# Moving the scan's states, the values' transposes and a modulation panel within the first block of a two-block kernel

## The chip, the cores and the metric

The kernel runs on one core of a Trainium2 chip. The metric is the device time of one execution in microseconds (us). Times below come from one profiled execution or from the timed runs, and the text says which. TensorE is called PE, its weight loads PEld, VectorE DVE, ScalarE ACT, GpSimd POOL; SP is the engine that issues the DMAs of the weights.

## What is computed

The program chains two blocks. The change is in the first, a hybrid layer over 512 tokens of width 1024 with a context of 256 tokens: a modulated norm, one projection, neighbourhood attention and a bidirectional state-space scan side by side, an output projection and a gated feed-forward part. Cut to what the change touches:

```python
mod = silu(c) @ ada_w + ada_b                  # six vectors of 1024: shifts, scales, gates
p = h @ w_in                                   # columns q, k, v | z | xbc | dt
attn = neighbourhood_attention(q, k, v, kc, vc, rpb, rows)   # softmax over a window and the context
dt = softplus(dt_raw + dt_bias);  a = -exp(a_log)            # step sizes, rates
xbc = silu(depthwise_conv(xbc));  xs, bm, cm = split(xbc)
# the scan, in chunks of 128, forward and backward:
cum = cumsum(dt * a);  w_end = exp(cum[-1] - cum) * dt
states = einsum("jgn,jge,jgep->gepn", bm, w_end, xs)         # one per chunk and direction
h = exp(cum[-1]) * h + states                                # carried from chunk to chunk
y = (cb * decay * dt) @ xs + (cm * exp(cum)) @ h_in;  y = rms_norm((y + d * xs) * silu(z))
x = x + g1 * (concat(attn, y) @ w_out);  x = x + g2 * conv_glu(modulate(rms_norm(x)))
```

## The kernel before

**Panels.** Every weight matrix is cut into panels of 128 columns. A panel is loaded by DMA into one of three raw buffers, ACT writes its high part (`wh`, L653), DVE or POOL the rest (`wl`, L663), and PE forms three products for each of 8 slices of the contraction (high x high, high weights x low input, low weights x high input; L685), so 24 products a panel. Panels alternate between two weight slots and two pairs of accumulator banks; ACT or DVE takes the sum out of PSUM. The low part is first needed by the third product. In the first block come 4 panels q, 4 k, 4 v, 1 dt, 8 xbc, 4 z (the gate), then 8 wo (the output projection).

**Modulation.** The 32 panels of the modulation weights that aren't needed at the start travel in the same stream of raw buffers, one behind each projection panel (`panels_of`, two behind dt). POOL multiplies and adds one (four instructions, L972 to L981), or DVE from number 24 on (eight instructions, L958 and L961, `mod_by`); its column sum (`modset`, L865) is done by PE two panels later. A raw buffer is loaded again when its reader is done, and SP issues the loads in the order of the stream.

**One plan, five streams.** `put` appends steps to one list, `plan`; afterwards each engine runs over that list and emits its own part of every step, with waits on semaphores. So the order within an engine is the order of `put`, and an instruction that waits holds all behind it on its engine. Small results use a ring of four banks (4 to 7) or of eight.

**Work beside the panels.** `gemm(..., every=5)` calls `tick` at products 1, 6, 11, 16 and 21 of a panel. `tick` advances the generator `na_order`, which puts one step and yields. If it yields `ALONE`, the slot is full; otherwise `tick` is called once more. The 12 panels xbc and z hold 60 slots. `drain` runs what is left. `na_order` holds 16 units of attention (scores, turn of the probabilities, values), then the rates of the scan (`rates1`) and the silu of xbc (`silu_x`, two halves of 128 x 3076).

**Around it.** Behind dt PE turns the step sizes (`dt_turn`), softplus goes back and forth between DVE and ACT, and nine tiles of values are turned by PE (`turn_v`, L1123) and copied by ACT (L1264) into `V`. `V` lies where the step sizes' scratch `wdt` and `sp_t` lay, so its copies, and the DMA of the mask, wait for `sp_done`. `zero_pads` clears DVE's convolution buffers. Behind each xbc panel DVE runs a convolution (L1333 to L1338).

**The scan.** After z: `turn_s` turns a chunk's x and B (PE L1571, L1575; ACT copies them), `state` (PE L1589) multiplies B with x times the end weights (DVE L1738 forward, POOL L1910 backward), `run` (DVE L1746 to L1756) carries the state on into `Hst`. Ten states, six chunks (4 and 5 are the context). Then `prep` (PE L1599, L1606), `masked` and `yout` work off eight pairs of chunk and group; this stage is called the next stage below. `Hst` shares memory with the projection's inputs `hh` and `hl`, which z still reads.

Of the kernel before, what the change touches and what calls it, by code (L numbers as in the profile page):

```python
# [120 lines left out]
def program(nc, io):  # L121
    ctx = ExitStack()
    with ctx:
# [177 lines left out]
        def mod_by(n):  # L301
            return "mod_dve" if n >= 24 else "mod_part"
# [688 lines left out]
        wdt = sbt(sc, "wdt", [128, S + CT])  # L991
        sp_t = [sbt(sc, f"spt{i}", [128, 96]) for i in range(4)]
        sc.close()
        sc = ExitStack()
# [20 lines left out]
        def natural(src):  # L1015
# [4 lines left out]
            "softplus": "sp_in/0 sp_out/0 sp_in/1 sp_out/1 sp_done", "turn_v": "turned copied",  # L1020
            "na_scores": "biased scored maxed/0 maxed/1 exped/0 exped/1", "na_turn": "turned/0 turned/1 copied/0 copied/1 scaled",
            "na_values": "weighed copied scaled",
            "steps1": "act_fn scaled",
# [13 lines left out]
        def na_order():  # L1037
            for u in range(16 + 1):
# [14 lines left out]
            yield ALONE  # L1053
            yield ALONE
            put("silu_x", 1)
            yield ALONE

        gemm(("q",), then_first, feed=feed_first)
# [24 lines left out]
        def first_sync(sp, w):  # L1083
# [5 lines left out]
            def na_mask():  # L1089
                w.wait_ge(s.sp_done, at("sp_done", "softplus", 0))  # L1090
# [6 lines left out]
            return {"rope_tables": rope_tables, "na_mask": na_mask, "na_rel": na_rel}  # L1097

        def first_tensor(pe, w, held, free):
# [19 lines left out]
            def turn_v(i):  # L1119
                b, = bank("turn_v", i)  # L1120
                held(b)
                for m in range(4):
                    ins = pe.transpose(ps[b][:, 128 * m:128 * m + 128], vT[:, m, V_AT[i]:V_AT[i] + 128], C("ident"))  # L1123
                ins.then_inc(up("turned", "turn_v", i), 1)
                free[b] = [(s.copied, at("copied", "turn_v", i))]
# [26 lines left out]
            def na_values(u):  # L1152
# [8 lines left out]
                for k, v in enumerate((*VI[j], 7, 8)):  # L1161
                    for e in range(2):
# [5 lines left out]
            return {"rope": rope, "dt_turn": dt_turn, "turn_v": turn_v, "na_scores": na_scores, "na_turn": na_turn,  # L1168
# [37 lines left out]
        def first_scalar(ac, w):  # L1206
# [85 lines left out]
        def first_vector(dv, w, st):  # L1292
# [98 lines left out]
        Hst = sbt(sb_, "Hst", [128, 2, 4, 512])  # L1391
# [7 lines left out]
        CBm = [sbt(sb_, f"CBm{i}", [128, 2, 128]) for i in range(2)]  # L1399
        seg = [sbt(sb_, f"seg{i}", [128, 512]) for i in range(2)]  # L1400
        Ms = [sbt(sb_, f"Ms{i}", [128, 512]) for i in range(4)]
        Cs = [sbt(sb_, f"Cs{i}", [128, 512]) for i in range(4)]
        yt = sbt(sb_, "yt", [128, 2, 128])
# [5 lines left out]
        ORDERS = [[4, 5, 0, 1, 2, 3], [5, 4, 3, 2, 1, 0]]  # L1409
        TRI = ["upper", "lower"]  # L1410
        STATES = [(d, ORDERS[d][n], n == 0) for n in range(5) for d in range(2)]
# [2411 lines left out]
```

## Time and profile before

| | us |
|---|---|
| timed runs, median of 3 (lowest, highest) | 2633.28 (2632.15, 2634.3) |
| the profiled execution | 2630.9 |
| its span (first to last instruction) | 2628.9 |
| busy in the span: PE, PEld | 2488.0 (95%), 2203.1 (84%) |
| busy in the span: DVE, ACT, POOL | 1351.1 (51%), 973.6 (37%), 961.3 (37%) |

The profile page also draws the span in 40 slices of 65.7 us. Each digit is a busy share in tenths; PEclk is the clock granted to TensorE, in tenths of its upper level (2.4 GHz). The first block's projection, attention and scan lie in slices 2 to 7.

```profile
PE   7989988999999999999999999999998998999997
DVE  4646577644534544454364354466654534644453
PEclk9999999999999999999999999999999998999998
```

A busy share of 95% over the whole span says nothing of one stage. The timeline of an engine gives start, duration, instruction and, in brackets, the idle time before it and what ended that.

### The profile page before, as it was taken

The numbers are of one execution on the slowest core, as the hardware profiler recorded it, in microseconds if no ns is written. First come the engines' busy times: TensorE is split into PE (matmuls) and PEld (weight loads), VectorE is DVE, ScalarE is ACT, GpSimd is POOL, SyncE is SP. The second block draws the span as 40 slices with busy tenths as digits, with TensorE's granted clock in tenths as the row PEclk, the third lists the DMA queues.
The fourth block names the chain that finished last, engine by engine and source line by source line (L and its number), as shares of the span: only waits on it lengthen the run. The fifth ranks groups of instructions, "written<-read, shape, count | busy, mean of one in ns | idle before, by whom it ended". The sixth has DMA issues, their size and how long they took to land.

```text
span 2628.9 us, 44461 instructions
## 1 busy us (share of the span) xinstructions
PE 2488.0 (95%) x19232; PEld 2203.1 (84%) x19232; DVE 1351.1 (51%) x2057; ACT 973.6 (37%) x1558; POOL 961.3 (37%) x553
## 2 busy tenths in 40 slices
PE   7989988999999999999999999999998998999997
PEld 5877676788887878878999999988988987989896
DVE  4646577644534544454364354466654534644453
ACT  5244453322323443424433333354333234333332
POOL 1754443344445222212445454500002114454544
PEclk9999999999999999999999999999999998999998
DMA  8432212333333211111223332312111002232321
GB/s 247 135 103 77 71 41 81 96 90 95 96 92 93 57 41 49 41 44 39 81 73 106 87 97 79 95 49 65 35 40 33 22 24 71 81 106 87 104 76 62
DMA packets 379858, 201.26 MB, mean 77 GB/s; under 512 B 6400, under 2 KB 377088, under 8 KB 379664
## 3 DMA queue, kind: packets, MB, share of 16 engines
q1 hardware_dynamic: 379664, 198.42, 26.6%
q8 instruction: 152, 2.49, 0.4%
q14 instruction: 42, 0.34, 0.0%
HBM read 196.30 MB, written 2.10 MB: 75 GB/s over the span
## 4 chain that ended last, share of the span: by engine, by line
PE 61%; DVE 12%; ACT 5%; issue 2%; POOL 2%; POOLq 0%; ACTq 0%; DVEq 0%
PE ps L685 48%; DVE t_ffy L2953 3%; DVE t_atq L2747 2%; ACT t_wh L653 1%; PE ps L2555 1%; PE ps L3188 1%; PE ps L2528 1%; DVE t_ffy L2956 1%; PE ps L2494 1%; PE ps L3207 1%; ACT t_ffy L2856 1%; PE ps L3211 1%; POOL t_wl L663 1%; DVE t_ainv L2775 1%; DVE t_wl L663 1%
## 5 line engine op out<-in xcount | busy, mean ns | idle before, releaser
L663 POOL TENSOR_TENSOR t_wl<-t_raw,t_wh 128x1024 fp32r<-128x1024 f32 (+2 forms) x196 | 443.4, 2263 | 810.2 <-ACT t_wh L653 810.1
L685 PE MATMUL ps<-t_hh,t_wh 128*128 128x264 f32 (+2 forms) x1712 | 402.8, 314 | 12.1 <-DVE t_dcq L2681 3.6
L653 ACT ACTIVATE t_wh<-t_raw 128x1024 fp32r<-128x1024 f32 (+2 forms) x253 | 255.4, 1012 | 415.0 <-PE ps L685 368.3
L685 PE MATMUL ps<-t_hh,t_wl 128*128 128x264 f32 (+2 forms) x1712 | 379.6, 300 | 4.7 <-POOL t_wl L663 3.1
L685 PE MATMUL ps<-t_hl,t_wh 128*128 128x264 f32 (+2 forms) x1712 | 376.9, 301 | 0.0
L685 PEld LDWEIGHTS ps<-t_hh,t_wh 128*128 128x128 f32 x1712 | 269.9, 191 | 36.9 <-issue 19.8
L685 PEld LDWEIGHTS ps<-t_hh,t_wl 128*128 128x128 f32 x1712 | 269.9, 190 | 21.4 <-issue 6.5
L685 PEld LDWEIGHTS ps<-t_hl,t_wh 128*128 128x128 f32 x1712 | 269.3, 191 | 14.6 <-issue 7.1
L2953 DVE SCALAR_TENSOR_TENSOR t_ffy<-t_ffp,t_vec,t_ffy 128x528 f32<-128x528 f32 (+1 forms) x88 | 176.1, 2002 | 178.8 <-ACT t_ffy L2856 178.8
L663 POOL TENSOR_TENSOR t_fwl<-t_raw,t_fwh 128x1024 fp32r<-128x1024 f32 (+1 forms) x72 | 167.9, 2333 | 152.2 <-ACT t_fwh L653 152.2
L685 PE MATMUL ps<-t_fhh,t_wl 128*128 128x512 f32 (+1 forms) x704 | 210.9, 340 | 2.9 <-POOL t_wl L663 2.8
L685 PE MATMUL ps<-t_fhh,t_wh 128*128 128x512 f32 (+1 forms) x704 | 210.5, 340 | 1.9 <-DVE t_fhl L1850 1.9
L685 PE MATMUL ps<-t_fhl,t_wh 128*128 128x512 f32 (+1 forms) x704 | 208.1, 338 | 0.0
L685 PEld LDWEIGHTS ps<-t_fhh,t_wl 128*128 128x128 f32 x704 | 120.0, 188 | 20.6 <-POOL t_wl L663 4.8
L685 PEld LDWEIGHTS ps<-t_fhh,t_wh 128*128 128x128 f32 x704 | 120.1, 188 | 20.1 <-DVE t_fhl L1850 3.4
L685 PEld LDWEIGHTS ps<-t_fhl,t_wh 128*128 128x128 f32 x704 | 119.5, 188 | 16.7 <-issue 0.4
L2998 POOL TENSOR_TENSOR t_ffl<-t_ffy,t_ffh 128x528 fp32r<-128x528 f32 (+1 forms) x44 | 57.8, 1314 | 132.3 <-ACT t_ffh L2865 132.3
L2681 DVE TENSOR_TENSOR t_ffp<-ps,t_rstd 128x264 f32<-128x264 f32 (+2 forms) x176 | 67.1, 422 | 74.6 <-PE ps L685 74.2
L663 DVE TENSOR_TENSOR t_wl<-t_raw,t_wh 128x1024 fp32r<-128x1024 f32 x57 | 78.8, 1384 | 49.0 <-ACT t_wh L653 49.0
L2747 DVE RECIPROCAL t_atq<-t_atq 128x528 f32<-128x528 f32 x16 | 55.2, 3453 | 70.8 <-ACT t_atq L2615 70.8
L653 ACT ACTIVATE t_fwh<-t_raw 128x1024 fp32r<-128x1024 f32 (+1 forms) x72 | 73.7, 1024 | 41.6 <-PE ps L685 36.8
L3634 POOL TENSOR_TENSOR t_dq<-t_dq,t_dRr 128x512 f32<-128x512 f32 (+1 forms) x10 | 11.4, 1137 | 200.9 <-PE ps L3158 200.9
(571 smaller groups left out, 5426.3 us busy)
## 6 DMA issues: line engine op xcount, KB each, us to landing
t_raw<-in_up SPq DMA_DIRECT2D x44, 512.0 KB, 3.9
t_raw<-in_up2a SPq DMA_DIRECT2D x44, 512.0 KB, 3.9
t_raw<-in_up2b SPq DMA_DIRECT2D x44, 512.0 KB, 3.9
t_raw<-in_attn_in SPq DMA_DIRECT2D x33, 512.0 KB, 4.1
t_raw<-in_dn_in SPq DMA_DIRECT2D x33, 512.0 KB, 4.1
t_raw<-in_ada_w SPq DMA_DIRECT2D x32, 512.0 KB, 4.1
t_raw<-in_w_in SPq DMA_DIRECT2D x25, 512.0 KB, 4.3
t_raw<-in_down SPq DMA_DIRECT2D x16, 512.0 KB, 4.1
```

The lines of the kernel that those rows point to most:

```text
L653: ac.activation(wh[slot_of[j]][:, 0:kc, :], raw[r % NRAW][:, 0:kc, :], ACT.Copy).then_inc(up("wh_cut", "cut", j), 1)
L663: eng.tensor_tensor(wl[slot_of[j]][:, 0:kc, :], raw[r % NRAW][:, 0:kc, :], wh[slot_of[j]][:, 0:kc, :].bitcast(F), SUB).then_inc(up(name, " ...
L685: ins = pe.matmul(ps[bank_of(j, i)][:, 0:tn], wt[slot][:, k, :], a[:, k, t0:t0 + tn], start=first, stop=last)
L2494: pe.matmul(ps[b][0:tn, 0:wide], aq[p % 3][64 * e:64 * e + 64, t0:t0 + tn], ak[p % 3][64 * e:64 * e + 64, a:a + wide], start=True, stop=False)
L2528: pe.matmul(ps[b][0:tn, 0:wide], ak[p % 3][64 * e:64 * e + 64, t0:t0 + tn], aq[p % 3][64 * e:64 * e + 64, q0:q0 + wide], start=True, stop= ...
L2555: ins = pe.matmul(ps[b][64 * e:64 * e + 64, lo - q0:lo - q0 + n], lhs, pT[e][0:tn, P_AT[k] + lo - t0:P_AT[k] + lo - t0 + n], start=k == 0, ...
L2681: ins = dv.tensor_tensor(a[part_, t0:t0 + tn], ap[part_, :], rstd[part_, t0:t0 + tn], MUL)
L2747: dv.reciprocal(tq[m][:, :], tq[m][:, :]).then_inc(up("inverted", "pair_norm", p, m), 1)
L2775: dv.reciprocal(inv[:, :], ps[bs_][:, 0:wide]).then_inc(up("inverted", "mixing", p, half), 1)
L2856: ac.activation(y[:, t], fp[par][:, t], ACT.Copy, scale=col(f"f{n}c0", f + NF * par)).then_inc(up("copied", kind, n, f), 1)
L2953: dv.scalar_tensor_tensor(out=y, in0=u[:, 1 + t0:1 + L], scalar=col(f"f{n}c1", f + NF * par), in1=y, op0=MUL, op1=ADD).then_inc(st.up(), 1)
L2998: po.tensor_tensor(low[:, k, t], ffn[n][2][2 * (f % 2)][:, t], high[:, k, t].bitcast(F), SUB).then_inc(up("lo_pool", "uconv1", n, f), 1)
```

## The change

1. `turn_v` moves ahead of softplus: three tiles, the turn of the step sizes, six tiles. The odd tiles (`turn_vd`) are copied by DVE. The step sizes' scratch moves to the memory of `zs`, so that neither these copies nor the mask's DMA wait for softplus. The exponential of `a_log` is a step of its own (`steps0`) ahead of softplus. PE's transposes wait for the last v panel alone.
2. `na_order` begins with two empty slots, loses one after the silu, puts both halves of the silu in one slot, and goes on with `turn_s`, `state` and `run`: turns 4, 5, 0, states 0 and 1, turn 3, states 2 and 3, turn 1, states 4 and 5, turn 2, states 6 to 9. They use the ring of four banks. `Hst` changes place with small buffers. The second gate panel too is copied raw and gets its silu later.
3. In the stream of panels one modulation panel moves from behind wo panel 1 to behind z panel 1. The numbers behind it shift by one up to there, so POOL does 25 of them and DVE 7.

```diff
@@ panels_of
-                for _ in range(2 if stage == "dt" else 1):
+                for _ in range({("dt", 0): 2, ("z", 1): 2, ("wo", 1): 0}.get((stage, m), 1)):
@@ mod_by
-            return "mod_dve" if n >= 24 else "mod_part"
+            return "mod_dve" if n >= 25 else "mod_part"
@@ program
-        wdt = sbt(sc, "wdt", [128, S + CT])
-        sp_t = [sbt(sc, f"spt{i}", [128, 96]) for i in range(4)]
+        zflat = rows_of(zs)
+        wdt = zflat[:, 0:S + CT]
+        sp_t = [zflat[:, S + CT + 96 * i:S + CT + 96 * i + 96] for i in range(4)]
@@ na_order
+            for _ in range(2):
+                yield ALONE
             for u in range(16 + 1):
...
             put("silu_x", 0)
-            yield ALONE
-            yield ALONE
             put("silu_x", 1)
             yield ALONE
+            for turned, ks in (((4, 5, 0), (0, 1)), ((3,), (2, 3)), ((1,), (4, 5)), ((2,), (6, 7, 8, 9))):
+                for c in turned:
+                    put("turn_s", c, banks=2, of=4)
+                    yield ALONE
+                for k in ks:
+                    sig.mark("pool_x" if k % 2 else "scaled", "state", k)
+                    put("state", k, banks=1, of=4)
+                    put("run", k)
+                    yield 1
...
-        put("dt_turn", banks=1)
+        for i in range(9):
+            put("turn_vd" if i % 2 else "turn_v", i, banks=1)
+            if i == 2:
+                put("dt_turn", banks=1)
+        put("steps0")
         put("softplus", 0)
         put("steps1")
-        for i in range(9):
-            put("turn_v", i, banks=1)
@@ na_mask (SP)
-                w.wait_ge(s.sp_done, at("sp_done", "softplus", 0))
+                w.wait_ge(s.took_a, at("took_a", "take", dt_j - 1))
@@ take_z, silu_z (ACT)
-                ac.activation(zs[:, m, :], spans[0][0], ACT.Silu if m else ACT.Copy).then_inc(up("took_a", "take", j), 1)
+                ac.activation(zs[:, m, :], spans[0][0], ACT.Silu if m > 1 else ACT.Copy).then_inc(up("took_a", "take", j), 1)
...
-                ac.activation(zs[:, 0, :], zs[:, 0, :], ACT.Silu).then_inc(up("act_fn", "silu_z"), 1)
+                ac.activation(zs[:, 0:2, :], zs[:, 0:2, :], ACT.Silu).then_inc(up("act_fn", "silu_z"), 1)
@@ turn_v (ACT), turn_vd (DVE)
-                w.wait_ge(s.sp_done, at("sp_done", "softplus", 0))
...
+            def turn_vd(i):
+                w.wait_ge(s.turned, at("turned", "turn_vd", i))
+                dv.tensor_copy(V[:, i, :], ps[bank("turn_vd", i)[0]][:, :]).then_inc(up("scaled", "turn_vd", i), 1)
@@ the scan after z
-        for turned, ks in (((4, 5), (0, 1)), ((0,), (2, 3)), ((3,), (4, 5)), ((1, 2), (6, 7, 8, 9))):
-            for c in turned:
-                put("turn_s", c, banks=2, of=8)
-            for k in ks:
-                sig.mark("pool_x" if k % 2 else "scaled", "state", k)
-                put("state", k, banks=1, of=8)
-                put("run", k)
```

## Rows read from the trace of the kernel before

**Rows 1.** The page's first line.

```profile
span 2628.9 us, 44461 instructions
```

**Rows 2.** Windows: stretch, length, busy time by engine, granted clock, DMA.

```profile
core 0: us, PE busy (x) PEld busy (x) DVE busy (x) ACT busy (x) POOL busy (x), PEclk, DMA share, GB/s
138.10:146.60 8.50, 8.50 (x51) 7.46 (x50) 1.44 (x2) 2.36 (x3) 6.01 (x5) 1.00 0.59 167
...
155.60:168.50 12.90, 7.81 (x42) 7.50 (x42) 6.26 (x17) 10.41 (x17) 0.00 (x0) 0.74 0.49 154
...
184.40:203.50 19.10, 16.98 (x110) 12.33 (x109) 11.36 (x20) 6.60 (x16) 13.27 (x14) 0.91 0.36 104
203.50:218.40 14.90, 14.55 (x97) 11.05 (x96) 9.75 (x17) 5.78 (x13) 11.20 (x9) 1.00 0.26 73
...
281.40:298.30 16.90, 15.22 (x108) 11.06 (x107) 10.45 (x19) 6.64 (x16) 6.22 (x8) 1.00 0.23 64
298.30:312.40 14.10, 11.84 (x74) 7.94 (x72) 9.54 (x17) 5.70 (x13) 9.75 (x7) 1.00 0.27 76
312.40:323.00 10.60, 10.18 (x81) 8.18 (x80) 5.40 (x14) 5.50 (x13) 1.42 (x2) 1.00 0.37 100
...
328.80:334.60 5.80, 5.80 (x27) 4.72 (x26) 1.44 (x2) 3.19 (x3) 0.00 (x0) 1.00 0.76 207
334.60:362.60 28.00, 18.57 (x79) 14.32 (x79) 21.19 (x32) 8.36 (x16) 9.52 (x7) 0.82 0.18 52
...
425.80:437.80 12.00, 7.92 (x30) 6.08 (x29) 9.34 (x22) 2.80 (x4) 1.81 (x1) 0.86 0.45 129
```

**Rows 3.** Timeline of PE behind the dt panel: start, us, instruction, [idle before, releaser].

```profile
157.82 0.75 PE L1114 MATMUL ps<-t_cst,t_wdt 32*128 32x32 f32 x6 [2.18 <-ACT t_wdt L1227]
...
164.74 4.05 PE L1123 MATMUL ps<-t_cst,t_vT 128*128 128x128 f32 x20 [2.91 <-ACT t_V L1264]
...
173.06 0.63 PE L1147 MATMUL ps<-t_cst,t_sco 128*128 128x128 f32 x4 [0.57 <-ACT t_sco L1271]
```

**Rows 4.** Timeline of ACT in the same stretch.

```profile
161.03 0.28 ACT L1177 ACTIVATE t_spt<-t_spt 128x96 f32<-128x96 f32 x1
...
164.09 3.25 ACT L1264 ACTIVATE t_V<-ps 128x512 f32<-128x512 f32 x6 [1.24 <-DVE t_dts L1204]
```

**Rows 5.** Timeline of DVE in the same stretch.

```profile
165.28 0.70 DVE L1328 MEMSET t_sqb<- 128x771 f32 x1
170.59 0.42 DVE L1349 SCALAR_TENSOR_TENSOR t_sco<-ps,t_nab 128x256 f32<-128x256 f32 x1 [4.60 <-PE ps L1136]
```

**Rows 6.** Timeline of PE, the attention's turns in two xbc panels.

```profile
182.83 1.04 PE L1147 MATMUL ps<-t_cst,t_sco 128*128 128x128 f32 x8
...
289.61 0.63 PE L1147 MATMUL ps<-t_cst,t_sco 128*128 128x128 f32 x4 [0.93 <-ACT t_sco L1271]
```

**Rows 7.** Timelines of DVE and ACT, from the rates to the first silu.

```profile
321.30 0.26 DVE L1721 TENSOR_SCALAR t_ncum<-ps 128x96 f32<-128x96 f32 x1 [1.13 <-PE ps L1559]
...
322.39 1.28 ACT L1248 ACT_TABLE_LOAD   x1
323.69 2.78 ACT L1248 ACTIVATE t_xbc<-t_xbc 128x3076 f32<-128x3076 f32 x1
```

**Rows 8.** Timelines of PE and DVE in the scan's states.

```profile
340.72 3.78 PE L1589 MATMUL ps<-t_Ms,t_Btm 128*128 128x256 f32 x8 [3.35 <-DVE t_Ms L1738]
...
350.72 1.97 PE L1589 MATMUL ps<-t_Ms,t_Btm 128*128 128x256 f32 x8 [2.18 <-issue]
...
353.86 0.68 DVE L1738 TENSOR_TENSOR t_Ms<-t_kT,t_wend 128x512 f32<-128x512 f32 x1
```

**Rows 9.** Timelines of ACT, DVE and PE at the third projection panel.

```profile
425.32 1.06 ACT L653 ACTIVATE t_wh<-t_raw 128x1024 fp32r<-128x1024 f32 x1 [2.69 <-PE ps L685]
...
427.18 2.67 DVE L961 SCALAR_TENSOR_TENSOR t_part<-t_raw,t_small,t_part 128x128 f32<-128x128 f32 x7
429.77 1.22 DVE L663 TENSOR_TENSOR t_wl<-t_raw,t_wh 128x1024 fp32r<-128x1024 f32 x1
...
431.04 0.79 PE L685 MATMUL ps<-t_mh,t_wl 128*128 128x512 f32 x1 [3.24 <-DVE t_wl L663]
```

More of the change, by code:

```diff
@@ L1019, in program @@
             "rope": "multiplied roped/1 roped/2 roped/3", "dt_turn": "turned scaled",
-            "softplus": "sp_in/0 sp_out/0 sp_in/1 sp_out/1 sp_done", "turn_v": "turned copied",
+            "softplus": "sp_in/0 sp_out/0 sp_in/1 sp_out/1 sp_done", "turn_v": "turned copied", "turn_vd": "turned scaled", "steps0": "act_fn",
             "na_scores": "biased scored maxed/0 maxed/1 exped/0 exped/1", "na_turn": "turned/0 turned/1 copied/0 copied/1 scaled",
             "na_values": "weighed copied scaled",
-            "steps1": "act_fn scaled",
+            "steps1": "scaled",
             "rates1": "multiplied/cum scaled/neg scaled/pos multiplied/tot scaled/raw exped/cd exped/we scaled/we",
@@ L1052, in na_order @@
             put("silu_x", 0)
-            yield ALONE
-            yield ALONE
             put("silu_x", 1)
             yield ALONE
+            for turned, ks in (((4, 5, 0), (0, 1)), ((3,), (2, 3)), ((1,), (4, 5)), ((2,), (6, 7, 8, 9))):
[7 more added lines that the diff above has]
+                    yield 1
+        ORDERS = [[4, 5, 0, 1, 2, 3], [5, 4, 3, 2, 1, 0]]
+        STATES = [(d, ORDERS[d][n], n == 0) for n in range(5) for d in range(2)]
+        SIGNALS.update({"turn_s": "turned/0 turned/1 copied/0 copied/1", "state": "multiplied", "run": "h_run"})
         gemm(("q",), then_first, feed=feed_first)
@@ L1117, in dt_turn, with turn_tile, turn_v @@
                 free[b] = [(s.scaled, at("scaled", "dt_turn"))]
-            def turn_v(i):
-                b, = bank("turn_v", i)
+            def turn_tile(kind, i):
+                b, = bank(kind, i)
                 held(b)
+                w.wait_ge(s.took_a, at("took_a", "take", dt_j - 1))
                 for m in range(4):
                     ins = pe.transpose(ps[b][:, 128 * m:128 * m + 128], vT[:, m, V_AT[i]:V_AT[i] + 128], C("ident"))
-                ins.then_inc(up("turned", "turn_v", i), 1)
-                free[b] = [(s.copied, at("copied", "turn_v", i))]
+                ins.then_inc(up("turned", kind, i), 1)
+                free[b] = [v_turned(i)]
+            def turn_v(i):
+                turn_tile("turn_v", i)
+            def turn_vd(i):
+                turn_tile("turn_vd", i)
             def na_scores(u):
@@ L1390, in program @@
         xtm = rows_of(kT).rearrange("p (c n) -> p c n", n=512)
-        Hst = sbt(sb_, "Hst", [128, 2, 4, 512])
+        CBm = [sbt(sb_, f"CBm{i}", [128, 2, 128]) for i in range(2)]
+        seg = [sbt(sb_, f"seg{i}", [128, 512]) for i in range(2)]
+        Cs = [sbt(sb_, f"Cs{i}", [128, 512]) for i in range(4)]
+        yt = sbt(sb_, "yt", [128, 2, 128])
+        sbt(sb_, "scan_pad", [128, 256])
         Btm = sbt(sb_, "Btm", [128, 6, 256])
@@ L1398, in program @@
         cdec = sbt(sb_, "cdec", [128, 6, 16])
-        CBm = [sbt(sb_, f"CBm{i}", [128, 2, 128]) for i in range(2)]
-        seg = [sbt(sb_, f"seg{i}", [128, 512]) for i in range(2)]
         Ms = [sbt(sb_, f"Ms{i}", [128, 512]) for i in range(4)]
-        Cs = [sbt(sb_, f"Cs{i}", [128, 512]) for i in range(4)]
-        yt = sbt(sb_, "yt", [128, 2, 128])
+        Hst = sbt(sb_, "Hst", [128, 2, 4, 512])
         sb_.close()
@@ L1425, in program @@
             "mix": "hi_set lo_pool",
-            "turn_s": "turned/0 turned/1 copied/0 copied/1",
             "prep": "multiplied/cb multiplied/0 multiplied/1 scaled/cb scaled/0 scaled/1",
             "decay_s": "exped/0 exped/1", "decay_c": "exped/0 exped/1 pool_x/0 pool_x/1", "masked": "scaled/0 scaled/1",
-            "x1": "pool_x", "state": "multiplied", "run": "h_run",
+            "x1": "pool_x",
             "yout": "weighed scaled/a0 scaled/a1 scaled/b",
@@ L1637, in mix, with steps0 @@
                               ACT.Copy).then_inc(up("hi_set", "mix", m), 1)
-            def steps1():
+            def steps0():
                 w.wait_ge(s.vec_in, 16)
-                ac.activation(small[:, 16:32], col("a_log", 0, 16), ACT.Exp).then_inc(up("act_fn", "steps1"), 1)
+                ac.activation(small[:, 16:32], col("a_log", 0, 16), ACT.Exp).then_inc(up("act_fn", "steps0"), 1)
             def rates1():
```

17 lines of the change are left out of this document (9 added, 8 removed).

## The prediction, made before the change was run

> **What bounds the kernel now.** The page gives one number to start from, the span of 2628.9 us [rows 1]; the profiled run lasted 2630.9, so 2.0 us lie around the span. The change touches only the first block, so I cut that stretch into stages with the windows view, one window per weight panel of TensorE (PE), each from the end of one panel to the end of the next [rows 2]. The reader is to compare a window's length with PE's busy time: a gate panel without other work takes 5.80 us with no idle time, so wherever a window's length exceeds its busy time, PE waits for somebody, and that somebody sets the time. Three places stand out: 155.6 to 168.5 (5.1 us idle, granted clock 0.74), the scan's states from 334.6 to 362.6 (9.4 us idle, 0.82) and the third projection panel, 425.8 to 437.8 (4.1 us idle, 0.86; a panel alone needs 5.8). Then I read PE's timeline in each for what ended the idle time [rows 3, 8, 9], and the timelines of ScalarE (ACT) and VectorE (DVE) for what those were doing. PE is in order: what waits in its stream stops the panels behind it.
>
> **Part 1, values turned early.** Before, PE stops 2.18 us for the copy of the step sizes and 2.91 us for the first copies of V, which wait on the end of softplus, and the transposes run slow [rows 3, 4]. Eight transposes take 1.04 us at full clock [rows 6], so a tile of four costs 0.5. After: three tiles at once from 155.6 to 157.1, a wait of 0.7 for the step sizes, their turn to 158.3, then six tiles, each as its bank comes free; ACT copies one in 0.54 [rows 4], DVE takes the odd ones, at about 0.6 (an estimate from its 512-wide operations of 0.68 [rows 8]). The last ends at 161.1, where the first xbc panel now starts, 7.4 us earlier than 168.5. One third more time for the copies would cost 0.6.
>
> **What comes late next.** The softplus chain now starts after the copies. ACT ends them at 161.7; a table load and the exp of a_log bring 163.2; Exp, DVE's add, a second load of 1.28 [rows 7] and Ln end at 165.1. From the end of Ln (161.3 before) DVE needed 4.7 us to the end of the two memsets at 166.0 [rows 4, 5], so DVE is free at 169.8. Behind it in DVE's stream stand the first scores. From their first operation to PE's first turn pass 2.5 us (170.59 to 173.06) [rows 3, 5]: turn at 172.2. PE, two empty slots later in its order than before, arrives at 161.1 + 17 products of 0.354 (24 in 8.5, a panel with nothing beside it [rows 2]) + scores 1.1 = 168.3. It idles 3.9 us, then 1.0 between the two halves, and resumes at 174.0 with 17 products done; before it resumed at 174.8 with 7. Lead: 0.8 + 3.5 = 4.3 us. I charge 2.0 for the clock: after waits of 2.2 and 2.9 us the transposes ran at half speed (20 in 4.05 us against 8 in 1.04) [rows 3, 6]; bounds 0 and 2.7. Lead 2.3.
>
> The Trainium skill ("ScalarE: Activation LUTs", What ACT_TABLE_LOAD costs) puts a drain of about 1380 ns behind each load of 1283. Two loads stand in this chain, so by the page PE would idle 2.8 us longer and the sum end 2.8 higher. The trace shows a load of 1.28 us that starts at 322.39 and the silu at 323.69, 0.02 us behind it [rows 7]; I leave the page's drain out.
>
> **The attention beside the panels.** Shifted by two slots, the attention meets the convolutions at other places. A panel that begins with scores right behind a convolution idles most (2.1, 1.1 and 1.7 us in three cases, two of them in the rows, the first with the clock at 0.91), one that begins with a turn or with values 0.2 to 0.5 (four cases, one in the rows) [rows 2]. There are two scores-first panels among the xbc panels instead of three, but the first gate panel becomes one. There PE arrives sooner: 289.6 is 8.2 us after its panel's start at 281.4 [rows 6], and in a gate panel the same place is reached in 5.8 (12 products of 0.233, scores, values, a modulation column). So 2.4 + 0.8 us of wait and 1.7 for the clock, against 2.3 idle now [rows 2]. Summed over the nine panels: idle and clock 11.2 against 10.6, a loss of 0.6. The rates' PE work (0.8) moves behind gate panel 2. Gate panel 2 then ends at 323.0 - 2.3 - 0.8 + 0.6 = 320.5.
>
> **Part 2, states beside gate panels 3 and 4.** Count of slots: 12 panels give 60; 2 empty, 48 of attention, 1 rates, 1 silu leave 8: turns of chunks 4, 5, 0 in panel 3, four half steps with states 0 to 5 and turns 3, 1 in panel 4. Turn 2 and states 6 to 9 are left behind it.
> Panel 3: the rates on DVE stand behind the panel's low part, which ends 2.6 us after the panel starts (cut 1.06, low part 1.22 [rows 9], and their waits), then 1.1 from DVE's first operation to the end of ACT's two exps (321.30 to 322.39), 1.28 table, twice 2.75 silu [rows 7]: with the start-up the silu ends at 10.6. PE reaches the first turn, which waits for it, at 3.9 and idles 6.7 us. Behind it: three turns (0.8 to 0.9 each), 12 products of 0.233, 1.9 for the clock. Panel 3 lasts 18.3 instead of 5.8.
> Panel 4: state 0 needs DVE's product with the end weights, which stands behind the low part of the first projection panel (2.6) and takes 0.7: 3.35, PE idles 2.5. A pair of states costs 1.97 at full and 3.78 at half clock [rows 8]. 3.35 + 3.78 + 5 products half slow 1.65 + turn 0.9 + 1.16 + pair 1.97 + 1.16 + 0.9 + 1.16 + 1.97 + 0.47 = 18.5. DVE keeps up: 0.7 + four operations of 0.7 are less than the 5.2 us between pairs.
> Behind it: DVE ends run 5 (0.5), multiplies a modulation panel (2.95, as at 427.18), makes the low part of projection panel 2 (1.15): the factor for state 6 starts 4.6 us after the panel. Before, from that factor at 353.86 to PE's next stage at 362.6 were 8.8 us, with waits for GpSimd and half clock; GpSimd is now early, which gives 6.4 at full clock, 8.1 at half; I take 7.6. Sum 12.2 instead of 28.0.
> Together 18.3 + 18.5 + 12.2 = 49.0 against 39.6 now. The next stage starts at 369.5, **6.9 us later** than 362.6. Bounds of the 49.0: 43.6 with the clock at its upper level, 55 with it low. The moved work itself is worth nothing here: PE does it in either place, and it is the waits that count.
> Hidden: the mask and the bias table (their DMAs no longer wait for softplus on SP's queue and are needed at 169.8), the loads of raw panels (each has over 5 us), POOL's extra modulation product (its last step ends about 1 us into panel 4, ahead of state 1's factor). Uncovered, each costs up to its 4 to 5 us.
>
> **Part 3, projection panel 3 ahead of the modulation.** PE waits 3.24 us for its low part, because DVE multiplies a modulation panel first (2.67 + 0.3) [rows 9]; then it runs at half clock. Without it the low part ends at 428.1, PE waits 0.4, and the panel ends at 433.1 instead of 437.8: **4.7 us less**. Its raw panel is there (the cut ran at 425.32 already). Next late would be panel 4's low part at 432.9, in time by 0.2 plus three products. Bounds 3 and 5.
>
> **Sum.** +6.9 - 4.7 = +2.2: span 2631.1, run 2633.1; against the median of the runs 2633.28 + 2.2, **2635.5 us**.
>
> **Rivals.** (a) *The clock stays up.* PE idled 2.18 us before 350.72 and went on at full clock (8 in 1.97) [rows 8]; so did it after 1.8 us in the first gate panel [rows 2]. If none of the new waits costs clock: -2.0 (first turn), -2.5 (second scores-first panel and gate panel 1), -1.9, -2.3, -1.2 (panels 3, 4 and behind) = -9.9, that is 2625.6. Against it: the half speed behind 2.9 us and at 340.72 behind 3.35 [rows 3, 8], and the new waits are as long or longer. (b) *Slower: the low clock lasts.* After 6.7 us idle in panel 3 and 2.5 in panel 4, PE's clock stays at 0.5 from the silu wait to the second pair of states: 5.5 us of work at half instead of 2, +3.3, and +2.5 in panel 4: 2641.3. It decides if a low stretch lasts over 5 us; the longest single row at half speed now is 4.05 us [rows 3]. (c) *The projection panel gains nothing*, because the scan's end or the cut is later still: 2640.2. Against it: cut at 425.32, end of the modulation product 429.8, low part right behind it [rows 9].
>
> **Chances.** A change of under 0.2% (5.3 us) can't be told from none here. Forecast 0.53, (a) 0.15, (b) 0.25, (c) 0.07. The range, 2627 to 2641.5, takes in nearly all of (a) and (b). Some of the forecast's own spread (about 4 us from the sizes of the waits) falls beyond 2638.5 and 2628.0: faster 0.16, same 0.51, slower 0.33.
>
> **What would show it.** The first xbc product near 161.1, PE idle near 4 us before the first turn; gate panel 2's end at 320.5; an idle stretch of 6 to 7 us in gate panel 3 ended by the silu of ACT, one of 2 to 3 us in panel 4 ended by DVE's factor; the next stage's first products near 369.5; projection panel 3 in 7.4 us from 425.8's counterpart instead of 12.0. Wrong if PE doesn't wait for the silu, or if the low clock costs much more or less than 1.9 a time.

## The result and the profile after

The changed kernel takes 2649.38 us (median of 4 runs, 2647.21 to 2651.17), the kernel before beside it 2633.79 (4 runs, 2632.15 to 2637.37). The ratio is 1.0058, its 95% interval 1.0046 to 1.0071: 15.6 us slower. The forecast was 2635.5 with a range up to 2641.5, so it was wrong by 13.9 us, 7.9 beyond the end of the range. One of the four executions of kernel 2 below took 4763 us, for a reason that no trace shows, and isn't in that kernel's median. The profiled execution took 2651.17, its span 2649.3:

```profile
span 2649.3 us, 44457 instructions
```

The windows of the changed kernel answer to [rows 2]: the stretch ahead of the first turn, gate panels 1 to 4, the stretch behind them up to the next stage, and projection panel 3. Columns are as there.

```profile
163.00:177.90 14.90, 7.13 (x38) 5.21 (x37) 11.21 (x22) 5.88 (x9) 6.69 (x7) 0.90 0.15 57
297.80:318.20 20.40, 15.23 (x85) 9.39 (x84) 13.00 (x19) 5.82 (x14) 7.17 (x6) 0.83 0.20 53
318.20:329.80 11.60, 11.60 (x88) 8.54 (x87) 5.34 (x13) 6.33 (x15) 6.71 (x6) 1.00 0.33 92
329.80:348.20 18.40, 10.54 (x52) 8.77 (x51) 3.63 (x7) 10.92 (x13) 5.17 (x4) 0.81 0.19 57
348.20:366.00 17.80, 14.31 (x67) 11.78 (x66) 10.35 (x15) 3.54 (x8) 4.49 (x4) 0.90 0.20 59
366.00:383.00 17.00, 8.31 (x26) 6.11 (x25) 13.68 (x21) 4.64 (x6) 5.53 (x4) 0.60 0.22 63
...
446.20:453.80 7.60, 6.43 (x30) 4.96 (x29) 7.08 (x14) 2.79 (x4) 1.37 (x1) 1.00 0.24 71
```

Four of these windows are longer than PE's busy time by 5 us or more. The timeline of PE says who ends the idle time in each: the turn of the probabilities waits for ACT's exp twice, the first turn of the scan for the silu, the states for DVE's factors. They answer to [rows 3, 8, 9].

```profile
177.91 1.08 PE L1170 MATMUL ps<-t_cst,t_sco 128*128 128x128 f32 x4 [7.78 <-ACT t_sco L1295]
...
308.49 1.08 PE L1170 MATMUL ps<-t_cst,t_sco 128*128 128x128 f32 x4 [4.87 <-ACT t_sco L1295]
...
341.49 1.08 PE L1590 MATMUL ps<-t_cst,t_xbc 128*128 128x128 f32 x4 [7.86 <-ACT t_xbc L1273]
...
352.74 3.48 PE L1608 MATMUL ps<-t_Ms,t_Btm 128*128 128x256 f32 x8 [3.49 <-DVE t_Ms L1757]
...
374.19 3.75 PE L1608 MATMUL ps<-t_Ms,t_Btm 128*128 128x256 f32 x8 [7.24 <-DVE t_Ms L1757]
```

The next stage's first product starts at 382.96 instead of 362.6. The third projection panel's low part now comes 1.0 us into the panel instead of 3.9 (at 448.53, after a wait of 0.33 us), and the panel's window is 7.6 us long instead of 12.0.

To compare many kernels I use one landmark that all have, ACT's table load ahead of the first silu of the feed-forward, and call it the end of the first block:

```profile
489.01 1.28 ACT L1697 ACT_TABLE_LOAD   x1
```
```profile
504.93 1.28 ACT L1716 ACT_TABLE_LOAD   x1
```

It stands at +15.9 us in the changed kernel, which is the measured loss of 15.6; what the profiled run shows beyond it (a span longer by 20.4) arises far behind the change and is taken up at the end.

### The profile page after: what moved, and what is told of

It reads as the page before. It is cut to its first block, busy times and chain, and to the rows that moved or that the text cites. A ratio compares the mean times of both kernels' runs of the same rounds, so it can differ in the third digit from the quotient of the medians.

```text
span 2649.3 us, 44457 instructions
## 1 busy us (share of the span) xinstructions
PE 2496.8 (94%) x19232; PEld 2208.7 (83%) x19232; DVE 1357.1 (51%) x2053; ACT 972.8 (37%) x1554; POOL 968.3 (37%) x557
## 4 chain that ended last, share of the span: by engine, by line
PE 61%; DVE 12%; ACT 5%; issue 2%; POOL 1%; POOLq 0%; ACTq 0%; DVEq 0%
PE ps L685 48%; DVE t_ffy L2972 3%; DVE t_atq L2766 2%; ACT t_wh L653 1%; PE ps L2574 1%; PE ps L3207 1%; PE ps L2547 1%; DVE t_ffy L2975 1%; PE ps L2513 1%; PE ps L3226 1%; ACT t_ffy L2875 1%; PE ps L3230 1%; POOL t_wl L663 1%; DVE t_ainv L2794 1%; DVE t_wl L663 1%
```

## The experiments

Theory 1: the loss is made of waits of PE in its own order, two of them made by GpSimd running beside VectorE (behind dt, and at the last convolution), the others by the silu and by VectorE's queue ahead of the factors. Theory 2: the parts themselves are near zero and the clock, or the moved work, costs. The table gives medians, their difference to the kernel before on the same chip (2632.29 for the first four kernels, 2631.50 for the next four, 2631.75 for the last four), the ratio with its interval, and the shift of the end of the first block, from one profiled execution each. The medians have intervals of 2 to 5 us to either side, so for pieces of 2 to 4 us I rely on the timelines and the landmark. The landmark has a spread of its own: in the eleven kernels with part 1's order, PE turns the step sizes at 159.0 to 160.4 us, ahead of everything in which these kernels differ from each other, so a difference of under 1.4 us between two landmarks says nothing.

| kernel | median | difference | ratio [interval] | first block |
|---|---|---|---|---|
| whole change | 2649.38 | +15.6 | 1.0058 [1.0046, 1.0071] | +15.9 |
| 1 part 1 alone | 2637.47 | +5.2 | 1.0015 [1.0005, 1.0024] | +4.2 |
| 2 part 2 alone | 2647.20 | +14.9 | 1.0057 [1.0040, 1.0073] | +15.7 |
| 3 part 3 alone | 2633.39 | +1.1 | 1.0005 [0.9995, 1.0014] | -2.5 |
| 4 whole, GpSimd held behind softplus | 2644.92 | +12.6 | 1.0049 [1.0032, 1.0065] | +11.9 |
| 5 part 1 with that hold | 2633.01 | +1.5 | 1.0006 [0.9997, 1.0016] | -0.9 |
| 6 whole, GpSimd held behind the convolution | 2644.49 | +13.0 | 1.0053 [1.0036, 1.0070] | +13.8 |
| 7 whole, modulation 25 on GpSimd | 2645.28 | +13.8 | 1.0054 [1.0039, 1.0069] | +11.9 |
| 8 whole, five empty slots behind the silu | 2638.96 | +7.5 | 1.0025 [1.0013, 1.0036] | +6.5 |
| 9 parts 1 and 3, both holds | 2631.00 | -0.8 | 0.9996 [0.9987, 1.0005] | -3.0 |
| 10 the same, four empty slots | 2626.26 | -5.5 | 0.9978 [0.9970, 0.9987] | -4.5 |
| 11 the same, modulation 25 on GpSimd | 2623.68 | -8.1 | 0.9971 [0.9960, 0.9981] | -8.4 |
| 12 whole change with all cures | 2627.42 | -4.3 | 0.9983 [0.9972, 0.9993] | -7.5 |

**1. Part 1 alone.** The states go back behind z, the stream of panels is as before.

```diff
-            for turned, ks in (((4, 5, 0), (0, 1)), ((3,), (2, 3)), ((1,), (4, 5)), ((2,), (6, 7, 8, 9))):
-                ...                                   # in na_order
+        for turned, ks in (((4, 5), (0, 1)), ((0,), (2, 3)), ((3,), (4, 5)), ((1, 2), (6, 7, 8, 9))):
+            ...                                       # behind drain, of=8
-                for _ in range({("dt", 0): 2, ("z", 1): 2, ("wo", 1): 0}.get((stage, m), 1)):
+                for _ in range(2 if stage == "dt" else 1):
```

> Part 1 of the change alone: values turned ahead of softplus, two empty slots at the start of the attention (and the second gate panel copied raw); states behind the gate panels and modulation panels where they were. Theory 1 (the wait that was taken from the mask's DMA lets GpSimd's bias and modulation work run beside softplus on VectorE, whose small operations stretch): 5 to 6 us slower than before, 2639 to 2640; the first turn of the attention finds PE idle for 7 to 8 us, and softplus's last seven VectorE operations take 5 to 6 us instead of 2.6. Theory 2 (this part is as forecast, the loss of the whole change sits in the moved states): 1 to 2 us faster than before, first turn with PE idle for 4 us.

Measured +5.2 us. A step of which I forecast a gain of 2.3 us costs. PE waits 8.3 us before the first turn:

```profile
179.21 1.09 PE L1163 MATMUL ps<-t_cst,t_sco 128*128 128x128 f32 x4 [8.29 <-ACT t_sco L1288]
```

**2. Part 2 alone.** The values stand behind softplus again, with `sp_done` ahead of the copies and of the mask; the stream of panels is as before.

```diff
+        put("dt_turn", banks=1)
+        put("softplus", 0)
+        put("steps0")
+        put("steps1")
         for i in range(9):
-            put("turn_vd" if i % 2 else "turn_v", i, banks=1)
-            if i == 2:
-                put("dt_turn", banks=1)
-        put("steps0")
-        put("softplus", 0)
-        put("steps1")
+            put("turn_v", i, banks=1)
...
-                w.wait_ge(s.took_a, at("took_a", "take", dt_j - 1))
+                w.wait_ge(s.sp_done, at("sp_done", "softplus", 0))
                 sp.dma_start(mask[:, :, :], ...)
```

> Part 2 alone: the scan's turns and states 0 to 5 beside gate panels 3 and 4, with the two empty slots; values turned and copied behind softplus as before, modulation panels where they were. Theory 1 (PE waits for the silu and for VectorE's factors, and VectorE's long queue behind the last gate panel meets GpSimd's work): 13 to 16 us slower than before, 2647 to 2650, with 7 to 8 us idle before the first turn of a chunk and 7 us before state 6. Theory 2 (as forecast, the moved states cost 9 us): 8 to 10 us slower, 2642 to 2644.

Measured +14.9 us: this part alone is the size of the whole loss. The three parts measured singly (5.2, 14.9 and 1.1 us) add up to more than the whole change; kernels 1 and 2 share the two empty slots at the head of the attention and the second gate panel that is copied raw, so their losses can't be added. PE waits 6.60 us for the silu where I expected 7 to 8, and 7.24 before state 6. Its gate panels 3 and 4 and the stretch behind them take 17.8, 14.9 and 18.1 us:

```profile
325.70:343.50 17.80, 11.20 (x53) 9.37 (x51) 2.37 (x7) 10.94 (x13) 2.52 (x4) 0.81 0.22 60
343.50:358.40 14.90, 12.41 (x63) 10.39 (x62) 8.83 (x14) 3.52 (x8) 1.04 (x1) 1.00 0.12 36
358.40:376.50 18.10, 8.85 (x27) 6.43 (x25) 14.49 (x23) 4.64 (x6) 5.54 (x4) 0.62 0.21 59
```

Together 50.8 us where the kernel before needs 39.6 [rows 2]: 11.2 of the 15.7 us by which the landmark moved. Of the rest, 2.7 stand at the end of gate panel 2 already (325.7 for 323.0), 1.3 of them from ahead of the step sizes' turn, and 1.8 come in behind the scan.

**3. Part 3 alone.**

```diff
-                for _ in range(2 if stage == "dt" else 1):
+                for _ in range({("dt", 0): 2, ("z", 1): 2, ("wo", 1): 0}.get((stage, m), 1)):
-            return "mod_dve" if n >= 24 else "mod_part"
+            return "mod_dve" if n >= 25 else "mod_part"
```

> Part 3 alone: one modulation panel moves from behind projection panel 2 to behind gate panel 2. Both theories: 4 to 5 us faster than before, 2629, because PE no longer waits 3.2 us at projection panel 3 and keeps its clock. The rival that the gain was never there: within 1 us of before.

Measured +1.1 us, with an interval of -1.3 to +3.7: both theories missed. The wait itself went as forecast, 3.24 us in [rows 9] and 0.34 here:

```profile
430.11 0.50 PE L685 MATMUL ps<-t_mh,t_wl 128*128 128x512 f32 x1 [0.34 <-DVE t_wl L663]
```

From projection panel 3's first product to the landmark it wins 4.4 us (from +2.0 to -2.5), so the step is right. Of the +2.0, 1.5 arise in gate panels 1 and 2: 0.9 in the first, where no wait is longer than before but the granted clock is 0.89 instead of 1.00, and 0.6 in the second, which has one more product on GpSimd beside it (its values wait 0.97 us for VectorE instead of 0.42). The shift of the profiled run is -2.5 us at the landmark and +2.5 at its end, so the rest is lost in the second block (last section).

**4. The whole change, GpSimd held.** GpSimd's first addition of bias and mask waits for the end of softplus, and so does all behind it in its order.

```diff
                 w.wait_ge(s.mask_in, 16)
+                if u == 0:
+                    w.wait_ge(s.sp_done, at("sp_done", "softplus", 0))
```

> The whole change, and GpSimd's first bias step waits for softplus to end. Theory 1 (GpSimd's work beside softplus stretches VectorE's chain): 4 to 6 us faster than the change without this wait, 2643 to 2645; softplus's VectorE operations are back at 0.2 to 0.3 us each, PE idle before the first turn is 3 to 4.5 us instead of 7.8. Theory 2 (the operations are slow because their scratch lies elsewhere in memory, or because the chain is longer than I worked out): no difference or slower, 2649 to 2652.

Measured +12.6 us against +15.6 (4.5 between the bare medians), and 4.0 by the landmark. The two timelines of the tail of softplus show why. In the whole change, VectorE and then GpSimd:

```profile
168.68 0.68 DVE L1224 TENSOR_TENSOR t_zs<-t_zs 128x96 f32<-128x96 f32 x1
169.39 0.68 DVE L1226 TENSOR_TENSOR t_zs<-t_zs 128x96 f32<-128x96 f32 x1
170.00 0.72 DVE L1227 TENSOR_SCALAR t_zs<-t_zs 128x96 f32<-128x96 f32 x1
170.75 1.87 DVE L1229 TENSOR_TENSOR t_dts<-t_zs 128x96 f32<-128x96 f32 x1
172.74 1.23 DVE L1733 SCALAR_TENSOR_TENSOR t_dA<-t_dts,t_small 128x96 f32<-128x96 f32 x1
174.07 0.70 DVE L1351 MEMSET t_sqb<- 128x771 f32 x1
```
```profile
167.80 2.85 POOL L1406 TENSOR_TENSOR t_nab<-t_rstd,t_namask 128x256 f32<-128x256 f32 x4 [11.03 <-DMA t_rstd<-in_rpb]
...
170.62 1.90 POOL L972 TENSOR_TENSOR t_raw<-t_raw,t_small 128x1024 f32<-128x1024 f32 x1
```

and with the hold, VectorE and PE:

```profile
168.62 0.26 DVE L1224 TENSOR_TENSOR t_zs<-t_zs 128x96 f32<-128x96 f32 x1
...
169.33 0.26 DVE L1229 TENSOR_TENSOR t_dts<-t_zs 128x96 f32<-128x96 f32 x1
169.70 0.26 DVE L1735 SCALAR_TENSOR_TENSOR t_dA<-t_dts,t_small 128x96 f32<-128x96 f32 x1
```
```profile
173.90 0.63 PE L1170 MATMUL ps<-t_cst,t_sco 128*128 128x128 f32 x4 [3.71 <-ACT t_sco L1295]
```

Five operations of 0.20 to 0.26 us take 0.68, 0.68, 0.72, 1.87 and 1.23 when GpSimd works beside them, 3.9 us more in a chain that PE waits for. The 1.87 is about as long as GpSimd's own 1.90 beside it. The memset, which reads nothing, keeps its 0.70. The scratch lies in the same place in both kernels, so the expectation's second theory, which blamed its place, is out. By the Trainium skill ("SBUF — State Buffer", SBUF: two separate sides) GpSimd and a VectorE operation with two inputs in SBUF, or in a mode that uses two ports, take a shared pair of ports by an exclusive lock for a whole instruction; by that rule the small operation waits for the whole of the large one, and the rows agree.

**5. Part 1 with that hold.** The edit of 4 in the kernel of 1.

> Part 1 alone, and GpSimd's first addition of bias and mask waits for the end of softplus. Theory 1 (GpSimd beside VectorE's small operations is what made part 1 dear): the first turn's idle falls from the 8.3 us of part 1 alone to 3.7 as in the whole change with the same hold, the first block ends 4 to 5 us sooner than in part 1 alone, so the run is 0 to 1 us below the kernel before, about 2631.5 to 2632.5. Rival (what part 1 costs lies in the two empty slots and the shifted attention, and the hold only moves the wait): within 1 us of part 1 alone, about 2637.

Measured +1.5 us against +5.2 (interval -0.8 to +4.2, where I expected -1 to 0), and 5.1 less by the landmark, 1.3 of which stand there before the step sizes' turn. PE idles 3.70 us before the first turn instead of 8.29. So the hold removes the loss of part 1, and what is left of its gain can't be told from nothing.

**6. The whole change, GpSimd held behind the last convolution.** Modulation panel 22 is the one that part 3 brings into gate panel 1.

```diff
                 w.wait_ge(raw_in[r % NRAW], 16 * (r // NRAW + 1))
+                if n == 22:
+                    w.wait_ge(s.conved, at("conved", "conv", 7))
                 po.tensor_tensor(x[:, :, :], x[:, :, :], ...
```

> The whole change, and GpSimd's modulation panel 22, the one that part 3 brings beside the last xbc convolution, waits for that convolution. Theory 1: VectorE's three operations of the convolution take 0.7, 1.0 and 1.0 us again instead of 2.3, 1.9 and 1.4, TensorE's wait in gate panel 1 falls from 4.9 to 2.1 us, and with the clock back the time falls by 2.8 to 4.5 us against the whole change, to about 2645 to 2646.5. Rival (the convolution is late for another reason, or the product given back later meets something else): within 1 us of 2649.4.

Measured +13.0 us against +15.6 (4.9 between the bare medians), and 2.1 by the landmark. VectorE's convolution in the whole change, with GpSimd's product beside it, and then the same with the hold and PE behind it:

```profile
300.49 2.26 DVE L1357 TENSOR_SCALAR t_xbc<-t_sqb,t_vec 128x769 f32<-128x769 f32 x1
302.78 1.92 DVE L1359 SCALAR_TENSOR_TENSOR t_xbc<-t_sqb,t_vec,t_xbc 128x769 f32<-128x769 f32 x1
304.74 1.36 DVE L1362 SCALAR_TENSOR_TENSOR t_xbc<-t_sqb,t_vec,t_xbc 128x769 f32<-128x769 f32 x1
```
```profile
299.44 2.88 POOL L972 TENSOR_TENSOR t_raw<-t_raw,t_small 128x1024 f32<-128x1024 f32 x1
```
```profile
302.12 0.67 DVE L1359 TENSOR_SCALAR t_xbc<-t_sqb,t_vec 128x769 f32<-128x769 f32 x1
302.83 1.02 DVE L1361 SCALAR_TENSOR_TENSOR t_xbc<-t_sqb,t_vec,t_xbc 128x769 f32<-128x769 f32 x1
303.88 1.02 DVE L1364 SCALAR_TENSOR_TENSOR t_xbc<-t_sqb,t_vec,t_xbc 128x769 f32<-128x769 f32 x1
```
```profile
307.28 0.63 PE L1172 MATMUL ps<-t_cst,t_sco 128*128 128x128 f32 x4 [2.06 <-ACT t_sco L1297]
```

5.5 us against 2.7, and PE's wait falls from 4.87 to 2.06. Gate panel 1 takes 16.8 us instead of 20.4, and 16.8 too in kernel 2, which doesn't have part 3. Of these 3.6 us, 2.8 are the shorter wait; the rest is clock, and it doesn't come each time: kernels 4 and 8, with waits of 4.87 and 4.90 us there, take 19.0 at a granted clock of 0.91, the whole change 20.4 at 0.83. The landmark shows less than 3.6 because this run was 1.6 us later when the panel began (299.36 for 297.75).

**7. The whole change, modulation panel 25 on GpSimd.**

```diff
-            return "mod_dve" if n >= 25 else "mod_part"
+            return "mod_dve" if n >= 26 else "mod_part"
```

> The whole change, with modulation panel 25 on GpSimd instead of VectorE. Theory 1 (behind gate panel 4 the factor of state 6 stands behind 3.3 us of modulation on VectorE and 2.1 of low part): TensorE's wait before state 6 falls from 7.2 to 4 us or so, the time by about 3 us, to 2646. Rival (a product on GpSimd stretches VectorE's low part and the factors there, so that the queue gets no shorter): the wait stays above 6 us and the time within 1 us of 2649.4.

Measured +13.8 us against +15.6 (4.1 between the bare medians), and 4.0 by the landmark. In the whole change VectorE has 3.34 us of modulation, 2.06 of low part and then the factor of state 6; GpSimd multiplies beside it:

```profile
367.27 3.34 DVE L961 SCALAR_TENSOR_TENSOR t_part<-t_raw,t_small,t_part 128x128 f32<-128x128 f32 x7
370.53 2.06 DVE L663 TENSOR_TENSOR t_wl<-t_raw,t_wh 128x1024 fp32r<-128x1024 f32 x1
372.51 1.52 DVE L1757 TENSOR_TENSOR t_Ms<-t_kT,t_wend 128x512 f32<-128x512 f32 x1
```
```profile
369.41 2.10 POOL L1929 TENSOR_TENSOR t_Ms<-t_kT,t_wend 128x512 f32<-128x512 f32 x2 [9.82 <-ACT t_kT L1671]
371.47 3.47 POOL L1917 TENSOR_TENSOR t_qT<-t_kT,t_dts 128x512 f32<-128x512 f32 x2
```
```profile
367.94 1.23 DVE L663 TENSOR_TENSOR t_wl<-t_raw,t_wh 128x1024 fp32r<-128x1024 f32 x1 [0.28 <-ACT t_wh L653]
369.08 0.68 DVE L1757 TENSOR_TENSOR t_Ms<-t_kT,t_wend 128x512 f32<-128x512 f32 x1
```
```profile
369.91 3.65 PE L1608 MATMUL ps<-t_Ms,t_Btm 128*128 128x256 f32 x8 [2.34 <-DVE t_Ms L1757]
```

The product gone, low part and factor fall into a time in which GpSimd is idle and take 1.23 and 0.68 us instead of 2.06 and 1.52. PE's wait falls from 7.24 to 2.34, 4.9 us, more than the 3.3 of the product itself.

**8. The whole change, five empty slots behind the silu.**

```diff
             put("silu_x", 1)
             yield ALONE
+            for _ in range(5):
+                yield ALONE
```

> The whole change with five more empty slots between the silu and the first turn of the scan: the three turns come at the end of gate panel 4, all states behind it. Theory 1 (the loss lies in TensorE's waits in its own order: for the silu, 7.9 us, for the factors, 3.5 and 7.2): gate panel 3 takes 5.8 us again, panel 4 about 9, the rest 25 to 26, together 41 instead of 53.2, and the time falls by 10 to 12.5 us, to 2637 to 2639. Rival (most of the loss is the clock and follows the moved work wherever it stands): 4 us or less, above 2645.

Measured +7.5 us against +15.6, 8.1 less (10.4 between the bare medians) and 9.5 by the landmark: the largest single piece of the loss. PE's wait for the silu falls from 7.86 us to 1.84, and no state stands in gate panel 4:

```profile
341.22 0.63 PE L1592 MATMUL ps<-t_cst,t_xbc 128*128 128x128 f32 x4 [1.84 <-ACT t_xbc L1275]
```

Gate panels 3 and 4 and the stretch behind them take 6.5, 10.0 and 26.6 us, together 43.1 (expected 41) instead of 53.2. The slots don't act on the silu's wait alone: PE waits 5.04 us before state 0, where the whole change waits 3.49, and 2.3 at most before any later state, where the whole change waits 7.24 before state 6. So the 10 us are those of moving the states back behind the gate panels, and what the silu's wait alone is worth isn't separated from the factors' waits and the clock.

**9 to 11. Parts 1 and 3 without part 2.** Kernel 9 has both holds, 10 has four empty slots at the head of the attention instead of two, 11 has modulation panel 25 on GpSimd besides.

```diff
         def na_order():
-            for _ in range(2):
+            for _ in range(4):
                 yield ALONE
```

> Parts 1 and 3 with the two holds on GpSimd (first addition of the bias behind softplus, modulation panel 22 behind the last xbc convolution), the scan's states back behind the gate panels. Theory 1 sums from the single runs in the first block: part 1 with its hold -0.9, the third projection panel -4.5, and up to +1.5 for the further product on GpSimd in gate panel 2: 3 to 5 us below the kernel before, 2627 to 2629. Rival (what is won in the first block is given back in the second, as part 3 alone did, whose first block ended 2.4 us sooner and whose run wasn't shorter): within 1.5 us of the kernel before.

> As the run before it in this call, with four empty slots ahead of the attention instead of two. Theory 1: TensorE idles 3.7 us before the first turn with two empty slots; two more hold ten products of 0.35 us, so that wait goes, and 2 to 4 us more are won, 2624 to 2626. Rival (shifted by two more slots the attention meets the convolutions elsewhere and the scores-first panels give it back): within 1 us of the run with two.

> As the run before it in this call, with modulation panel 25 on GpSimd. Theory 1: the first state's factor stands behind VectorE's product of 2.7 us; without it TensorE's wait of 3.3 us before state 0 shrinks to 1 or less and 2 to 3 us more are won, about 2622 to 2624. Rival (the product on GpSimd delays its own factors of the states): nothing won, the wait moves to the next pair.

Kernel 9 wins 3.0 us in the first block but 0.8 by the medians (interval -3.4 to +1.3), less than expected. Kernel 10 is 5.5 us below the kernel before (ratio 0.9978); PE's wait before the first turn, 3.70 us in kernel 9, is 0.46. The 4.7 us between the medians of kernels 9 and 10 can't be put down to the two slots alone: at the third projection panel kernel 10 stands 3.2 us before kernel 9 (425.24 for 428.45), 1.1 of them from before the step sizes' turn, by the landmark 1.5, and the two profiled runs also differ by 4.1 us in a stretch of the second block (last section). Kernel 11 is 8.1 us below (0.9971), and PE's wait before state 0, 3.35 us in kernel 10, is 1.43 in kernel 11, now for ACT's copy.

**12. The whole change with all cures**: the edits of 4, 6, 7 and 8 together.

> The whole change, states beside the gate panels included, with every cure of the single runs: the two holds, modulation panel 25 on GpSimd, five empty slots behind the silu. The single runs moved the end of the first block by -4.0, -2.1, -4.0 and -9.5 us from +15.9. Theory 1 (the waits lie apart and their cures add up): -3 to -5 us against the kernel before, 2627 to 2629. Rival (they overlap): 2630 or more.

Measured -4.3 us against the whole change's +15.6. By the landmark the four cures were worth 4.0, 2.1, 4.0 and 9.5 us one by one, 19.6, and 23.4 together (21.1 and 23.2 counted from the step sizes' turn). So the waits lie apart, and curing one doesn't merely uncover another. The median is 3.7 us above that of kernel 11, which leaves part 2 out, but has four empty slots at the head of the attention instead of two; the landmarks differ by 1.0. So no run here shows a gain or a loss of a cured part 2 by itself, and with the five slots only its turns stand beside the gate panels, not its states.

## Why the prediction was wrong

Its sum was for the start of the next stage: 369.5 us; it is 382.96, 13.5 us later, and the run is 13.9 over the forecast. The step that failed is one term: the forecast put GpSimd's work at nothing as long as it came in time, and took VectorE's durations from rows beside which GpSimd was idle. In three places the two run side by side and TensorE waits for VectorE: 3.5 us at the first turn, 3.6 in gate panel 1 and about 2.8 behind gate panel 4, some clock included. The kernel before had shown the price already, 1.65 us for a product of 128 x 96 that takes 0.26 in kernel 3, where GpSimd is idle beside it:

```profile
322.41 1.65 DVE L1727 TENSOR_TENSOR t_wend<-t_wend,t_dts 128x96 f32<-128x96 f32 x1 [0.49 <-ACT t_wend L1647]
```
```profile
322.04 1.90 POOL L972 TENSOR_TENSOR t_raw<-t_raw,t_small 128x1024 f32<-128x1024 f32 x1 [8.82 <-DMA t_raw<-in_ada_w]
```

Going through the steps:

- **Ahead of the change.** The dt panel ends 1.6 us later in this profiled run, which the change has no part in: kernel 3, with the old order there, has +1.3 at the same place. 1.6 of the 13.5 us.
- **Part 1, the start of xbc**: forecast 5.5 us after dt, measured 162.66 against 157.19, 5.5. Right.
- **The first turn**: forecast 3.9 us idle, measured 7.78. With GpSimd held it is 3.71. The chain was priced from rows in which GpSimd was idle [rows 5, and the zero under POOL in rows 2, 155.60 to 168.50]. It was idle because the mask's DMA waited 5.6 us for softplus, and with it the bias table's behind it on SP's queue, and the change removes that very wait. This is where the step failed first: the text lists mask and bias as hidden since they come in time, and asks only whether they come late, not what GpSimd does when they come early. Kernel 4 ends the xbc panels 3.5 us before the whole change (294.28 against 297.75).
- **The clock behind it**: I charged 2.0 us. The granted clock was 0.90 from 163.0 to 177.9 in the whole change, and 1.00 from 163.0 to 173.9 in kernel 4, where the wait was 3.7. There the second half of the turn takes 1.08 us instead of 0.63, so some clock is lost behind it; how much of the 2.0, the runs don't separate.
- **Gate panel 1**: forecast 2.4 + 0.8 us of wait, measured 4.87, and 20.4 us for the panel. Kernels 2 and 6, without GpSimd's further product there, have 2.05 and 2.06, and 16.8. The text says that this product is hidden because its last step comes in time. It is, but while it runs it stretches the convolution, and PE waits for what stands behind that. Kernel 6 against the whole change: 3.6 us in this panel, 0.8 of them clock. In the kernel before, too, a product beside this convolution stretched it, to 4.1 us.
- **Gate panel 3**: forecast 18.3 us (the terms written down for it add up to about 17.9), measured 18.4, with 7.86 us for the silu where I had 6.7. **Gate panel 4**: 18.5, measured 17.8. Right.
- **Behind panel 4**: forecast 12.2, measured 17.0. State 6's factor was to start 4.6 us after the panel and to take 0.7; it started 6.5 us after it and took 1.52. Between state 6's wait and the next stage the granted clock is 0.60; kernel 4 has the same two waits there (7.23 and 1.45), a clock of 0.77, and 15.0 us. So of the 4.8 us that were missing about 2.0 are the clock, and the rest is GpSimd beside VectorE again, as kernel 7 shows.
- **Part 3**: forecast -4.7 at its place, measured -4.4. Right at its place, but it costs 1.5 us in gate panels 1 and 2 by itself (kernel 3, 0.9 of them clock) and 3.6 in the whole change (kernel 6), which the sum didn't have.

The sum of the errors up to the next stage: 1.6 + 3.5 + 3.6 + 0.6 (not traced further) = 9.3 at the end of gate panel 2 (329.8 for 320.5), -0.6 in gate panels 3 and 4, +4.8 behind them: 13.5. The largest single term of the loss, the wait for the silu, was forecast in place and size; kernel 8 shows that taking the scan's turns and states out of its reach gives back 8 to 10 of the 15.6 us. That gate panels 3 and 4 together came out within 0.6 us is in part luck: the wait for the silu was 1.2 us longer than forecast, the one before state 0 1.0 longer, and other terms were smaller.

None of the rivals was what happened. Rival (b), the lasting low clock, named a larger loss but another cause. The line "Uncovered, each costs up to its 4 to 5 us" had about the right price for two of the hidden items (3.5 and 3.6 us), though for their coming late, and neither entered the range: had they, it would have reached about 2650. The range, said to take in nearly all of (a), also left out that rival's own price of 2625.6.

Of the Trainium skill's drain behind a table load ("ScalarE: Activation LUTs", What ACT_TABLE_LOAD costs), which I had left out, the changed kernel shows none either: the load at 165.26 takes 1.28 us and the Ln starts at 166.56.

```profile
165.26 1.28 ACT L1202 ACT_TABLE_LOAD   x1
166.56 0.28 ACT L1202 ACTIVATE t_zs<-t_zs 128x96 f32<-128x96 f32 x1
```

## What to carry to other kernels

When a wait is removed, ask not only whether the freed engine's results are needed earlier, but beside whom it will now run: a GpSimd product moved beside VectorE's chain costs that chain up to the product's own length, even if both results are in time. Durations read from a profile hold for the neighbours they had there; the chain of five tiny VectorE operations grew to four times its length here, the three of the convolution to twice theirs. And where PE keeps its order, put work behind a long silu or a factor only after enough slots to cover it: five empty slots were worth 8 to 10 us here.

## What the runs showed of the hardware

The second block, whose code no edit here touches, varies by up to 5 us in one stretch of some 154 us, with the same instructions and the same busy time on VectorE, ScalarE and GpSimd. The windows from one of its table loads to another, in the kernel before and in kernel 3:

```profile
1936.38:2090.36 153.98, 143.33 (x1854) 132.54 (x1853) 72.08 (x178) 41.87 (x60) 25.05 (x13) 0.96 0.11 29
```
```profile
1934.79:2092.80 158.01, 147.78 (x1854) 135.59 (x1853) 72.21 (x178) 41.88 (x60) 25.04 (x13) 0.92 0.11 28
```

It takes 153.8 to 154.0 us in the kernel before and in kernels 2, 5, 6, 8 and 10 (granted clock 0.96), 157.8 to 158.0 in kernels 1, 3, 9, 11 and 12 (0.92 to 0.94), 156.4 in the whole change (0.93) and 152.7 in kernels 4 and 7. One group of 32 products in it takes 1.99 us in the one and 3.75 in the other:

```profile
1967.42 1.99 PE L3099 MATMUL ps<-t_dog,t_cst 128*32 128x264 f32 x32
```
```profile
1965.74 3.75 PE L3099 MATMUL ps<-t_dog,t_cst 128*32 128x264 f32 x32
```

So 4 us are decided far from the change by where the half-speed stretches fall. They are 4.0 of the 5.0 us between the gain of kernels 3 and 9 in the first block (2.5 and 3.0) and their later end (2.5 and 2.0), and most of the spread of 5 to 10 us between runs of one kernel may be of this kind, though only one run of each was profiled, so whether an edit can steer it stays open. An experiment on 2 to 4 us of this kernel is better read at a landmark behind the edited stage, counted from one ahead of it, than at its end.
